# Sparse attention scores on the two halves of the array's rows, memory values between the attention units, and resets inside the recurrence gate, in a two-layer hybrid trunk

## The reference, cut to what matters

```
q, k_sel, k_win = rotary(q), rotary(k_sel), rotary(k_win)
cmp: softmax(q . kc)  over 31 compressed keys (kc = rotary(blocks of k_cmp @ w))
sel: softmax(q . k_sel), win: softmax(q . k_win), both causal over all 512 keys
out = gate0 * o_cmp + gate1 * o_sel + gate2 * o_win
```

```
r, i  = sigmoid(gates of the convolved input xc)
a     = exp(-8 * r * softplus(-lam)),  mult = sqrt(1 - a^2)
reset (position 0): a = 0, mult = 1
h_t   = a_t * h_(t-1) + mult_t * i_t * xc_t;   y = h * gelu(gate)
```

## Time and profile before

| | |
|---|---|
| three timed runs | 1552.11 us median (1547.91, 1552.11, 1553.23) |
| the profiled execution | 1547.39 us, its span 1545.6 us |
| mean granted PE clock | 0.992 of full |
| PE busy | 1509.6 us, 98% |
| POOL, ACT, DVE busy | 670.3, 609.3, 547.8 us |
| transfers | 147.04 MB, mean 95 GB/s |

### The profile page before, as it was taken

One profiled execution on the slowest core, in us unless ns is written; L12 is line 12 of the kernel. 1 busy time (PEld: TensorE's weight loads), 2 busy tenths in 40 slices (PEclk: granted clock), 3 DMA queues, 4 the chain that ended last, 5 costly groups with the idle time before them and its releaser, 6 DMA issues.

```text
span 1545.6 us, 21188 instructions
## 1 busy us (share of the span) xinstructions
PE 1509.6 (98%) x7762; PEld 1267.2 (82%) x7762; DVE 547.8 (35%) x928; ACT 609.3 (39%) x1207; POOL 670.3 (43%) x514
## 2 busy tenths in 40 slices
PE   8999999999999999999999999999999999999998
PEld 7878988878888888888887776778888888888886
DVE  2753673714360011110016179946435111011014
ACT  4345553344433333332233368733542333233221
POOL 5552002563445454445464544463243444544442
PEclk9999999999999999999999999999999999999999
DMA  9331001342224333333233522333122333332232
GB/s 246 116 113 56 1 1 30 95 156 70 94 77 143 102 96 95 96 94 102 96 118 92 151 76 62 109 116 96 62 89 90 96 96 96 102 95 95 96 100 90
DMA packets 113409, 147.04 MB, mean 95 GB/s; under 512 B 20278, under 2 KB 69808, under 8 KB 113328
## 3 DMA queue, kind: packets, MB, share of 16 engines
q1 hardware_dynamic: 113008, 145.87, 30.8%
q0 software_dynamic: 320, 0.08, 0.0%
HBM read 143.80 MB, written 2.10 MB: 94 GB/s over the span
## 4 chain that ended last, share of the span: by engine, by line
PE 92%; DVE 4%; ACT 2%; issue 1%; POOL 0%; DMA 0%; SPq 0%; DVEq 0%; ACTq 0%
PE ps L634 82%; PE ps L859 3%; PE ps L639 2%; PE ps L839 2%; PE ps L823 1%; PE ps L889 1%; DVE h L1672 1%; PE ps L785 0%; PE ps L815 0%; POOL w_lo L599 0%; DMA x_res<-in_x 0%; DVE y_lo L1362 0%; DVE tm L1669 0%; PE ps L825 0%; DVE ib_alt L1671 0%
## 5 line engine op out<-in xcount | busy, mean ns | idle before, releaser
L599 POOL TENSOR_TENSOR w_lo<-w_raw,w_hi 128x512 fp32r<-128x512 f32 (+1 forms) x452 | 604.6, 1346 | 846.3 <-ACT w_hi L1021 842.7
L1021 ACT ACTIVATE w_hi<-w_raw 128x512 fp32r<-128x512 f32 (+1 forms) x452 | 278.5, 626 | 576.5 <-PE ps L634 545.0
L634 PE MATMUL ps<-fm_hi,w_hi 128*128 128x512 f32 (+1 forms) x1096 | 418.7, 382 | 2.9 <-POOL w_lo L599 1.6
L634 PE MATMUL ps<-fm_hi,w_lo 128*128 128x512 f32 (+1 forms) x1096 | 416.4, 380 | 0.0
L634 PE MATMUL ps<-fm_lo,w_hi 128*128 128x512 f32 (+1 forms) x1096 | 416.4, 380 | 0.0
L634 PEld LDWEIGHTS ps<-fm_hi,w_hi 128*128 128x128 f32 x1096 | 206.1, 188 | 44.0 <-issue 2.7
L634 PEld LDWEIGHTS ps<-fm_hi,w_lo 128*128 128x128 f32 x1096 | 206.1, 188 | 39.5
L634 PEld LDWEIGHTS ps<-fm_lo,w_hi 128*128 128x128 f32 x1096 | 206.1, 188 | 39.3 <-issue 0.7
L1785 DVE TENSOR_TENSOR gf<-silu,ps 128x512 f32<-128x512 f32 x44 | 28.3, 684 | 431.6 <-ACT silu L1329 413.9
L1536 DVE SCALAR_TENSOR_TENSOR x_res<-x_res,ps 128x512 f32<-128x512 f32 x48 | 31.4, 684 | 275.4 <-PE ps L634 190.1
L634 PE MATMUL ps<-w_hi,g_lo 128*128 128x512 f32 x288 | 112.0, 389 | 0.0
(11 more groups left out here) (281 smaller groups left out, 2195.5 us busy)
## 6 DMA issues: line engine op xcount, KB each, us to landing
w_raw<-in_f_w_up SPq DMA_DIRECT2D x352, 128.0 KB, 2.1
w_raw<-in_f_w_down SPq DMA_DIRECT2D x88, 256.0 KB, 2.6
w_raw<-in_x_wkv SPq DMA_DIRECT2D x64, 256.0 KB, 3.1
w_raw<-in_o_w_in SPq DMA_DIRECT2D x40, 256.0 KB, 2.6
w_raw<-in_x_wq SPq DMA_DIRECT2D x32, 256.0 KB, 2.7
w_raw<-in_x_wo SPq DMA_DIRECT2D x32, 256.0 KB, 2.7
w_raw<-in_e_w_in SPq DMA_DIRECT2D x24, 256.0 KB, 3.3
w_raw<-in_o_w_out SPq DMA_DIRECT2D x20, 256.0 KB, 2.7
```

The lines of the kernel that those rows point to most:

```text
L599: nc.gpsimd.tensor_tensor(lo[:, :n], w_raw[:, c % RING, :n], hi[:, :n].bitcast(F32), ALU.subtract).then_inc(w_split, 1)
L634: last = nc.tensor.matmul(outp, lhsT, rhs, start=(clear and k == 0 and n == 0), stop=(k == steps - 1 and n == 2), skip_group_check=True)
L1021: nc.scalar.activation(w_pair(c)[0][:, :n], w_raw[:, s, :n], ACT.Copy).then_inc(w_rounded, 1)
```

## The change

Eight things are edited.

1. Scores. Queries are kept once, in f32, with heads g=0 and g=1 of a pair side by side, and split after the transpose into `qT_hi`, `qT_lo`. The pair's first head lies on rows 0 to 63, the second on rows 64 to 127, and so do the keys. Each pair gets three passes per head, alternating between the halves, into two banks, then two masks. A `cmp` unit has 16 products on half the rows where it had 8 on all.
2. Preparation. The high-part copies on ACT (line 1075), their subtraction on DVE (line 1455) and the doubling of the keys (lines 1450 and 1451) go. There are 16 query transposes for 32 and 8 key transposes for 16. `mix` comes before `k0_0`. The transposed compressed keys come before the last chunk of `k0_1`.
3. Memory values. `v0_0` and `v0_1` leave the norm (0,0). They become four groups `fv_0` to `fv_3` of 256 columns, whose 32 chunks are done between `scores(u + 2)` and `weigh(u)` (one or two per unit) in PSUM bank 7. The units' outputs now all use bank 6, so `weigh(u)` waits for the evacuation of unit u-1.
4. End of the attention. The output tiles are transposed inside the last two units and after the first chunk of `eout0`.
5. Norms. Tiles 0 and 1 are transposed in the midst of tiles 2 and 3 of the product (`k == steps - HELD + 2`). DVE does the low part of tile t-1 after normalising tile t. The norm (0,0) uses `early_half` of `q0_0`.
6. `oin2` does its last four chunks bank by bank, in the order 2, 3, 0, 1, and ACT takes each bank as it fills.
7. Resets. The gate r is raised to 1e32 at resets (`far`) before tanh and exp, which gives a = 0 and the multiplier 1; the products with `keep` at lines 1660 and 1669 go. Tanh waits for it.
8. The softplus moves from the start of layer 1 into layer 0, and the norm parameters of (0,0) are transferred later.

```diff
-                for hh in range(h0, h0 + heads):
-                    q, g, bank_ = qT[:, hh, qb * P:(qb + 1) * P], hh // GROUP, b0 + hh % 2
+                half = [slice(g * HD, (g + 1) * HD) for g in range(KV_HEADS)]
+                for i in range(h0 // 2, (h0 + heads) // 2):
...
-                        for i, k_ in enumerate((kT_hi, kT_lo)):
-                            nc.tensor.matmul(ps[:, bank_, c0:c0 + m], q, k_[:, BRANCHES.index(b), g, :m], start=(i == 0),
-                                             stop=False, skip_group_check=True)
+                        for s, (q_, k_) in enumerate(((qT_hi, kT_hi), (qT_hi, kT_lo), (qT_lo, kT_hi))):
+                            for g in range(KV_HEADS):
+                                nc.tensor.matmul(ps[:, b0 + g, c0:c0 + m], q_[half[g], i, tokens], k_[half[g], BRANCHES.index(b), :m],
+                                                 start=(s == 0), stop=False, skip_group_check=True)
...
+            def memory_values(i):
+                n, k = i // KT, i % KT
+                c = CHUNK0[f"fv_{n}"] + k
+                if k == 0 and n:
+                    evacuated(f"fv_{n - 1}")
+                pe.wait_ge(w_split, c + 1)
+                for m in range(MT):
+                    last = passes(ps[:, 7, m * FILL:(m + 1) * FILL], k, KT, [w_[:, :FILL] for w_ in w_pair(c)],
+                                  [x_[:, k, m * P:(m + 1) * P] for x_ in mem], False, clear=(m == 0))
...
             for u in range(len(UNITS)):
                 turn_probs(u)
                 if u + 2 < len(UNITS):
                     scores(u + 2)
+                for i in range(filled_until(u - 1), filled_until(u)):
+                    memory_values(i)
+                for t in {len(UNITS) - 2: (0, 1), len(UNITS) - 1: (2,)}.get(u, ()):
+                    turn_output(t)
                 weigh(u)
...
-                    turn_late(0, 0, fillers=(("v0_0", False), ("v0_1", False)))
-                product(f"q{l}_0", fm, SEQ, True, early=RING * l)
+                    turn_late(0, 0, "q0_0")
+                product(f"q{l}_0", fm, SEQ, True, early=RING)
...
+                    product("oin2", fm, SEQ, True, chunks=(0, KT - RING))
+                    for i, j in enumerate(OIN2_BANKS):
+                        for k in range(KT - RING, KT):
+                            last = passes(ps[:, o2 + j, :], k, KT, [w_[:, j * P:(j + 1) * P] for w_ in w_pair(c2 + k)],
+                                          [x_[:, k, :] for x_ in fm], True)
+                        if i < 3:
+                            last.then_inc(oin2_bank, 1)
...
+                            if j >= 2 and k == steps - HELD + 2 and by_tile != (DEPTH - 1, 2):
+                                turn_normed(*by_tile, j - 2)
...
+            def values_filled(n):
+                group_filled(act, f"fv_{n}")
+                nc.scalar.activation(v_mem[:, :, FILL * n:FILL * (n + 1)], ps[:, 7, :].rearrange("p (m c) -> p m c", c=FILL),
+                                     ACT.Copy).then_inc(evac_a, 1)
...
             for u in range(len(UNITS)):
                 turned_copy(u)
+                for n in range(filled_until(u - 2) // KT, filled_until(u - 1) // KT):
+                    values_filled(n)
+                round_weights(CHUNK0["fv_0"] + min(filled_until(u + 1) + 1, filled_until(len(UNITS))))
                 if u + 2 < len(UNITS):
                     act.wait_ge(summed, u + 1)
                     exps(u + 2)
...
+                            act.wait_ge(ra_reset, sum(s[1] for s in RG_SETS[:n]) + j + 1)
...
                             last = nc.scalar.activation(tm[:, j, :], RA[n][:, j, :], ACT.Tanh, scale=lru_c[:, 0, first + j:first + j + 1])
...
+                    def resets(n):
+                        for j in range(RG_SETS[n][1]):
+                            dve.wait_ge(evac_a, ACT_BEFORE[f"ra{n}"] + j + 1)
+                            nc.vector.tensor_tensor(RA[n][:, j, :], RA[n][:, j, :], far[:, :], ALU.max).then_inc(ra_reset, 1)
...
-                            nc.vector.tensor_tensor(a_, a_, keep[:, :], ALU.mult)
...
-                            settle(nc.vector.scalar_tensor_tensor(out=tm[:, j, :], in0=keep[:, :], scalar=0.0, in1=tm[:, j, :],
-                                                                  op0=ALU.is_equal, op1=ALU.max))
```

More of the change, by code:

```diff
@@ L116, in plan_groups @@
     g += [("ein0", KT, 4, 0), ("tm", 0, 4, 4), ("ein1", KT, 4, 0), ("ein2", KT, 4, 0), ("ein3", KT, 4, 0)]
-    g += [("k0_0", KT, 4, 0), ("mix", 0, 4, 4), ("tq0", 0, 2, 2), ("tq1", 0, 2, 2), ("tk", 0, 4, 4), ("cmp", 0, 3, 0), ("k0_1", KT, 4, 0), ("tkc", 0, 2, 0)]
+    g += [("mix", 0, 4, 4), ("k0_0", KT, 4, 0), ("tq", 0, 4, 4), ("tk", 0, 2, 2), ("cmp", 0, 3, 0), ("attn_", 0, 0, 0), ("k0_1", KT, 4, 0), ("tkc", 0, 0, 0)]
+    g += [(f"fv_{n}", KT, 1, 0) for n in range(D // FILL)]
     g += [("attn", 0, 0, 0), ("to", 0, 4, 4)]
@@ L443, in hybrid_trunk @@
         for name, steps, na, nd in PLAN:
-            if name == "k0_0":
+            if name == "mix":
                 TURNED["chan"] = len(TURNED) + 1
@@ L662, in token_tile @@
                                   [x_[:, kk, j * P:(j + 1) * P] for x_ in (hi, lo)], False)
-                for k in range(steps - HELD if by_tile else steps):
+                for k in range(*(chunks or (0, steps - HELD if by_tile else steps))):
                     c = CHUNK0[name] + k
@@ L753, in _ @@
             turn(ps[:, b0, V_CONVW:V_END], rows_rg[:, :], V_END - V_CONVW).then_inc(filled, 1)
-            product("k0_0", mem, MEM, True)
             b0 = begin("mix")
@@ L789, in _ @@
             last.then_inc(filled, 1)
-            product("k0_1", mem, MEM, True)
+            product("k0_1", mem, MEM, True, chunks=(0, KT - 1))
             b0 = begin("tkc")
-            pe.wait_ge(kcdup_ready, 1)
-            for g in range(KV_HEADS):
-                last = turn(ps[:, b0 + g, 0:NCMP], kc_dup[:, g, :, :].rearrange("p a d -> p (a d)"), NCMP)
-            last.then_inc(filled, 1)
-            evacuated("tkc")
+            pe.wait_ge(kc_rotated, 1)
+            turn(ps[:, b0, 0:NCMP], kc_tok[:, :, :].rearrange("n g d -> n (g d)"), NCMP).then_inc(filled, 1)
+            product("k0_1", mem, MEM, True, chunks=(KT - 1, KT))
+            pe.wait_ge(kc_ready, 1)
             pe.wait_ge(tables_ready, 3)
@@ L1099, in _ @@
             nc.scalar.activation(gates[:, :, :].rearrange("p t c -> p (t c)"), bank("cmp", 2)[:, 0:TT * GATES], ACT.Copy).then_inc(evac_a, 1)
+            round_weights(CHUNK0["k0_1"] + KT)
+            group_filled(act, "tkc")
+            nc.scalar.activation(kcT[:, 0:NCMP], bank("tkc", 0)[:, 0:NCMP], ACT.Copy).then_inc(kc_ready, 1)
             keys_evac(0, 1)
-            filled_by("tkc")
-            for g in range(KV_HEADS):
-                nc.scalar.activation(kcT[:, g, :], bank("tkc", g)[:, 0:NCMP], ACT.Copy).then_inc(evac_a, 1)
             def exps(u):
@@ L1598, in _ @@
                 if l == 0:
-                    norm(0, 0, ("eout0", "eout1"))
-                if l:
                     lam = chan[:, V_LAM:V_LAM + RT]
```

282 lines of the change are left out of this document (153 added, 129 removed).

## The result

The changed kernel takes 1541.89 us, median of 11 runs (1533.02 to 1544.34); the kernel before took 1552.04 beside it (1547.25 to 1557.59). The ratio is 0.9923 [0.9902, 0.9944], which makes it 11.9 us faster (10.2 between the two medians), where I had said 24.

The account below looks back on a forecast made before the run. PE, busy 98% of the span, was taken as the bound. The terms -4.5 - 6.6 + 21.9 - 24.5 - 8.0 = -21.7 took 1547.4 to 1525.7 us, stated as 1528 on the runs' scale; range 1516 to 1545.

Parts of the forecast that it names:

- Preparation: Before the compression: fewer transposes and DVE copies, against added waits of `cmp` and `k0_1`; sum -4.5 us.
- Scores: Attention scores: streams and loads of both row halves run in parallel, a 256-column pair 0.54 us for 0.72; -6.6 us.
- Memory values: Attention: 32 added chunks cost +23.0 us, partly filling idle time and avoiding half clock, with some waits added; sum +21.9.
- Norm (0,0): Two products leave this norm, with the 2.05 us gap between them and the half clock behind it; sum -24.5 us.
- Recurrence: Gaps at 870, 939.5 and 1002 go with half clock; late chunks in `oin3` and `oin4` add 3.2; sum -8.0 us.
- Half clock: Whole kernel: stretches of some 3.3 us at 1.2 GHz behind PE's gaps, each costing half of itself, 1.6 to 1.9 us.
- rival A: Scores and `cmp`: weight loads take turns; 1540 us, 1542 with the same half added; chance 0.15.
- rival C: Scores and `cmp`: halves don't overlap, PE empties at 64 half/full-row changes of 0.08 us; 1553 or 1556; chance 0.06.
- the 125 to 130: Sign of being right: the attention from its first mask to `eout0` takes 125 to 130 us, before 112.9.
- Rival B: Recurrence and attention: ACT's fixed order takes most of the recurrence's gain, adds half clock; 1533 or 1535; chance 0.13.
- D: No change: overlap holds, but gaps and half clock mostly return in other places; 1544 to 1550 us; chance 0.06.

Follow-up runs that it names:

- k4_full: Changed kernel with scores in two passes of all 128 rows a head, third pass left out (output wrong): 1532.35 us.
- k7_tk: Changed kernel with the key transposes put before the query transposes: 1539.28 us.
- k3_spread: Changed kernel with a pair's masks put behind its first and second pass, so more changes between half and full rows: 1567.01 us.
- k9_fullspread: On full-row scores (two passes of all 128 rows a head, third left out), first head's mask moved between the passes: 1533.92 us.
- k10_halfonly: Changed kernel with the causal mask added by the same 64 rows as the head's passes, the other rows' values left out: 1534.17 us.
- k1_group: Changed kernel with the masks of all pairs of a unit put behind all its passes: 1532.13 us.

## Why the prediction was wrong

The direction was right, and the places of the change's gains and costs were right but for one new gap in `oin2` and the half clock in the attention. The size was not. The median of 1541.9 is rival A's number (1542), but A's mechanism is not there: the two halves start together, as a rule under 10 ns apart. The agreement is luck. By the prediction's own steps:

- **Preparation** (-4.5): -4.2, from one profile each; the eight profiles with this preparation have it between 138.0 and 139.8, half clock out. The wait of `cmp` is 2.4 (2.5 said), that of `k0_1` 0.65 (0.7).
- **Scores** (-6.6): this step failed. The 22 units took 30.8 us before and 27.0 after (each from its first pass to what follows, half clock out), and the four `cmp` units 0.6 more, 2.11 for 1.87: -3.2. And this count leaves out the change into half rows ahead of each first pass. k4_full, which keeps everything else, gives the step as a whole: half rows make the attention 2.6 us longer, 9.2 away from -6.6. I took both streams and loads as parallel, rightly, but charged 0.08 us a pair for all changes. There are 64 between half and full rows in and around these units and 8 at the `cmp` units, at 0.15 each, some 11 us by that price where I had charged 2.6, and that is 8 of the 9.2. The compression could not show it: it changes once in 256 matmuls. I gave the changes a price in rival C (64 at 0.08, from the pass behind a mask) and set the rival aside as a whole because its other half, no overlap, was improbable. The two had nothing to do with each other. The Trainium skill (TensorEngine Tiling (Array Packing), "Key Properties") says that a change of the tiling mode drains the engine; the trace agrees with that, with 0.10 us more between the starts on both sides of a pair, and the runs give the change its price of 0.15.
- **Memory values** (+21.9, of it -1.6 clock): attention and scores leave +24.2 for it without clock, for 23.5 said. The near agreement is luck, because this remainder holds what the count of the scores leaves out. By k4_full, whose scores are the instructions of the kernel before, it is 129.6 - 111.2 = +18.4, 5.1 less than said; the same instructions take 35.7 us in its score and `cmp` units for 38.6, which is 2.9 of the 5.1 (my prices had made the units before 2.8 too cheap, 28.0 for 30.8); for the rest no single term is shown. The attention as a whole came to 132.2 us apart from the clock, outside the 125 to 130 that I had named as the sign of being right. The end waits 0.85 (1.0 said).
- **Norm (0,0)** (-24.5): -22.2 and 2.0 of half clock, as said.
- **Recurrence** (-8.0): the gaps at 870, 939 and 1002 closed as said, the late chunks in `oin3` and `oin4` cost 0.6 and 1.7 for 3.2 said. Missed was the gap of 2.9 in `oin2`. I counted what the bank-by-bank order gives to ACT and not what it asks of ACT: its last four chunks all rounded before the first bank ends, while they stand in the queue behind tanh and exponentials. Rival B named that mechanism for other chunks and priced it at +7.4; it got 0.13 and had part of the truth. So had D, by which gaps move instead of closing: 5.3 us of gaps stand in this stretch after the change.
- **Half clock.** I let it stand only behind gaps. In the profile of 1544 it takes 10 us more than in that of 1534, 5.1 of them more in the attention, where PE had been busy; k7_tk has the same stretch, k3_spread three times as much. The five profiles of kernels that change rows pair by pair lost 6.8, 1.7, 0, 6.8 and 20.5 us in the attention; the eight others (grouped masks, or full rows, or half rows alone) lost none; the kernel before lost 1.4 at the very end of its own. Over all runs, a mean granted clock of 0.991 or less stands in 15 of the 31 of those five kernels and in 1 of the 36 of the eight. That frequent changes of rows go with a falling clock is thus an association; how a change would do it is not shown. k3_spread against k9_fullspread excludes the masks' kind, and the 28 runs with half rows and grouped or halved masks exclude half rows as such. Why the same kernel shows it in some runs only stays open. So does one run of k4_full with 1538.5 at 0.991, which has no such changes, and two of k10_halfonly with 1536.5 at 0.993; none of the three was profiled.

The misses add up: 3.4 in the scores and 0.7 in the memory values (by k4_full 9.2 and -5.1, with the same sum), 1.7 in the recurrence, 0.9 in preparation and norm, 1.7 of half clock, from 1525.7 to 1534.1; the median run lies 7.8 above that by the clock. Rivals A and C (loads in turns, no overlap) are wrong by the starts shown, but C's term for the changes was right in kind and at 0.08 too low.

## What to carry to other kernels

Price a packed form of a matmul with the changes into and out of it, and count them: here 0.15 us each, so that three parallel passes of two heads between two changes were worth no more than four plain ones. Keep instructions of one form together across the whole unit; grouping the masks gave back 2.1 us of stream, and the clock of the attention was at full in every profile that had it. When an order is made finer on one engine, move the other engines' queues by hand to its first deadline: here a gap closed where ACT and DVE feed each other opened for the most part at the next place. And price a part of a change with a run that undoes that part alone: counted from its first instruction, it can hide a cost that lies ahead of it.

## What was new about the hardware

- A change between matmuls on 64 rows (two halves) and on 128 rows takes 0.15 us at full clock, measured in three ways (0.148 and 0.150 in units of k1_group, 0.155 in k3_spread); a change between f32 and bf16 operands in full rows takes 0.03.
- Two halves of the rows run f32 passes of 128 loaded columns fully side by side: 0.12 us for both at 256 columns, 0.23 at 512.
- The granted clock fell to half, from 2.4 to 1.2 GHz, for 13.7 and for 30.7 us in one piece, with no idle time of PE over 0.1 us in it or in the 18 us before it.
